# Mixer to MLP: x's first 512 columns are summed, weighted and turned while the output projection's second block runs

## The reference

```python
for l in range(2):
    h = rmsnorm(x, g_mix[l])
    # projections of h, three attention branches y_diff, y_mla, y_mem, and three gates
    merged = gates[:, :, 0] * y_diff + gates[:, :, 1] * y_mla + gates[:, :, 2] * y_mem
    x = x + merged @ w_out[l]                      # the output projection, 1024 x 1024

    u = rmsnorm(x, g_mlp[l]) @ w_mlp1[l]           # the MLP, 1024 x 4096
    x = x + jnp.square(jax.nn.relu(u)) @ w_mlp2[l]
```

## Time and profile before

| what | value |
|---|---|
| times of three executions | 2457.02, 2456.89, 2452.21 us |
| median | 2456.89 us |
| span of the profiled execution, first to last instruction | 2455.5 us |
| TensorE busy | 2387.7 us, 97% of the span |
| VectorE busy | 1521.6 us, 62% |
| ScalarE busy | 1188.3 us, 48% |
| GpSimd busy | 286.8 us, 12% |
| mean granted TensorE clock | 0.990 of full |

### The profile page before, as it was taken

How to read it: one execution, slowest core, us unless ns; L and a number is a source line. 1 busy time by engine, 2 the same in 40 slices (tenths; PEclk the granted TensorE clock), 3 DMA queues, 4 the chain that set the end, 5 groups by cost and what they waited for, 6 DMA issues and landing times.

```text
span 2455.5 us, 34969 instructions
## 1 busy us (share of the span) xinstructions
PE 2387.7 (97%) x14214; PEld 2058.1 (84%) x14214; DVE 1521.6 (62%) x2325; ACT 1188.3 (48%) x1782; POOL 286.8 (12%) x247
## 2 busy tenths in 40 slices
PE   8999999899999999999999999999999999999999
PEld 8987787689989977777899787787998877887997
DVE  6555556766556657666655677755665587656654
ACT  5444454344444445444444465554554455554543
POOL 1100010000000000000000122333100122333000
PEclk9999999999999999999999999999999999999999
DMA  7755645356656555544566655445566554445554
GB/s 231 210 190 174 166 119 150 118 154 189 184 172 185 181 192 174 169 141 153 165 181 204 197 162 147 125 125 163 177 193 210 182 163 125 126 139 162 174 187 146
DMA packets 269424, 411.69 MB, mean 168 GB/s; under 512 B 13770, under 2 KB 141658, under 8 KB 269264
## 3 DMA queue, kind: packets, MB, share of 16 engines
q1 hardware_dynamic: 262400, 389.59, 52.3%
q0 software_dynamic: 6432, 19.28, 3.0%
q10 hardware_dynamic: 432, 0.59, 0.1%
HBM read 408.31 MB, written 1.10 MB: 167 GB/s over the span
## 4 chain that ended last, share of the span: by engine, by line
PE 78%; DVE 13%; ACT 5%; issue 2%; POOL 1%; DMA 0%; SPq 0%; ACTq 0%; DVEq 0%
PE banks L1611 14%; PE banks L1613 14%; PE banks L1612 14%; PE banks L1637 10%; PE banks L1638 10%; PE banks L1646 9%; DVE w_lo L2192 3%; ACT w_hi L1890 3%; PE banks L1760 1%; PE banks L1700 1%; PE banks L1713 1%; DVE probs L2379 1%; DVE mx_merged L2867 1%; ACT probs L1998 1%; PE banks L1675 1%
## 5 line engine op out<-in xcount | busy, mean ns | idle before, releaser
L2192 DVE TENSOR_TENSOR w_lo<-w_raw,w_hi 128x1024 fp32r<-128x1024 f32 x688 | 838.7, 1224 | 690.4 <-ACT w_hi L1890 688.0
L1890 ACT ACTIVATE w_hi<-w_raw 128x1024 fp32r<-128x1024 f32 (+2 forms) x744 | 776.9, 1049 | 571.5 <-PE banks L1613 410.7
L1637 PE MATMUL banks<-xt_hi,w_hi 128*128 128x256 f32 x1920 | 479.4, 285 | 7.4 <-ACT xt_hi L1920 3.9
L1638 PE MATMUL banks<-xt_hi,w_lo 128*128 128x256 f32 x1920 | 477.9, 285 | 0.0
L1611 PE MATMUL banks<-w_hi,xt_hi 128*128 128x512 f32 (+2 forms) x1088 | 447.5, 411 | 11.5 <-DVE w_lo L2192 4.0
L1613 PE MATMUL banks<-w_hi,xt_lo 128*128 128x512 f32 (+2 forms) x1088 | 428.3, 394 | 0.0
L1612 PE MATMUL banks<-w_lo,xt_hi 128*128 128x512 f32 (+2 forms) x1088 | 427.4, 393 | 0.0
L1637 PEld LDWEIGHTS banks<-xt_hi,w_hi 128*128 128x128 f32 x1920 | 366.7, 191 | 10.0 <-issue 6.2
L1638 PEld LDWEIGHTS banks<-xt_hi,w_lo 128*128 128x128 f32 x1920 | 367.3, 191 | 0.0
L1646 PE MATMUL banks<-xt_lo,w_hi 128*128 128x256 f32 x1920 | 271.3, 283 | 0.0
L1611 PEld LDWEIGHTS banks<-w_hi,xt_hi 128*128 128x128 f32 x1088 | 206.7, 190 | 59.2 <-DVE w_lo L2192 6.4
(11 more groups left out here) (398 smaller groups left out, 2823.3 us busy)
## 6 DMA issues: line engine op xcount, KB each, us to landing
w_raw<-in_w_mlp SPq DMA_DIRECT2D x128, 512.0 KB, 3.7
w_raw<-in_w_in SPq DMA_DIRECT2D x104, 512.0 KB, 3.7
w_raw<-in_ffn_w_gate SPq DMA_DIRECT2D x88, 512.0 KB, 4.2
w_raw<-in_ffn_w_up SPq DMA_DIRECT2D x88, 512.0 KB, 4.3
w_raw<-in_ffn_w_down SPq DMA_DIRECT2D x88, 512.0 KB, 3.7
w_raw<-in_attn_w_in SPq DMA_DIRECT2D x72, 512.0 KB, 3.8
w_raw<-in_ret_w_in SPq DMA_DIRECT2D x64, 512.0 KB, 3.8
w_raw<-in_ret_w_out SPq DMA_DIRECT2D x16, 512.0 KB, 3.8
```

Source lines behind the costliest of these rows:

```text
L1637: pe.matmul(out[f], hi[:, cols], xh, start=(c == 0), stop=False)
L1638: pe.matmul(out[f], lo[:, cols], xh, start=False, stop=False)
L1890: act.activation(k.w_hi[i % SPLIT][:, 0:m], k.raw[i % RAW][:, 0:m], ACT.Copy).then_inc(*ev.mark(k.w_hi_made, ("w_hi", i)))
L2192: dve.tensor_tensor(lo, raw, hi.bitcast(F32), ALU.subtract).then_inc(*ev.mark(k.w_lo_made, ("w_lo", i)))
```

## The change

`last_plain` gets a mode `ahead`, used by the mixers only. In it the planner writes the steps of the next stage's first half between the tiles of the second block: behind T4 nothing, behind T5 the add and the gain of half 0, behind T6 the turn of half 0 and the add and the gain of half 1, behind T7 the turn of half 1. `feed` then finds that these are begun (`self.begun`) and starts at once with T8. So that the turned x can be written while T4 to T7 still read the turned merged rows, these lie in a place of their own (`mx_merged_t`, at 32 KiB of the work area, where the turned rows of the first branch lay before); they wait for the last tile that read these (`got["diff", "over"]`). No operation is added or removed, and the number of instructions is the same.

```diff
--- before.py
+++ after.py
@@ -456,7 +456,7 @@
         self.x_event = [[("x", 0, h, c) for c in range(2)] for h in range(HALVES)]
         self.tok_after = [[], []]
         self.xt, self.xt_after = None, []
-        self.pending, self.need_angles = None, True
+        self.pending, self.need_angles, self.begun = None, True, None
         self.memory, self.bias_heads, self.mem_after = None, {}, {}
         self.second_part = None
         self.out_scales, self.mem_scales, self.row_wide_of = {}, {}, {}
@@ -672,22 +672,23 @@
 
 
 
+    def begin(self, st):
+        return Transposed(f"x{st}", *self.xt_parts), self.next_gain(), {}
+
     def feed(self, between=None, order=""):
-        st, g = self.st, self.next_gain()
-        self.xt = Transposed(f"x{st}", *self.xt_parts)
+        st = self.st
+        begun, self.begun = self.begun, None
+        self.xt, g, gained = begun or self.begin(st)
         self.xt_scaled = True
-        gained = {}
 
         def part(half, c):
             if self.pending:
                 self.pending(half, c)
             by = "pool" if c and between else "dve"
-            self.step("gain", st, half, c, by, g, [self.x_event[half][c]] + self.tok_after[half])
-            gained[half, c] = "gain", st, half, c
+            self.gain_part(st, half, c, by, g, gained)
 
         def turned(half, c):
-            self.feed_turned = self.turn(lambda h, s: self.tok[:, h, s * P:(s + 1) * P], self.xt, half, [(4 * c + j, 4 * c + j) for j in range(4)],
-                                         [gained[half, c]], self.xt_after, order=order)
+            self.turn_part(self.xt, half, c, gained, order)
 
         def first():
             turned(0, 0)
@@ -710,6 +711,9 @@
             for half in range(HALVES):
                 self.step("rows", st, half, list(self.x_event[half]), self.stat(2), self.stat(1), self.row_means[half], "row_natural" if order else "row_scale")
 
+        if begun:
+            self.second_part = len(self.tiles) + 1, second
+            return
         part(0, 0)
         part(1, 0)
         if between:
@@ -720,6 +724,14 @@
                 self.held = list(range(SPLIT))
                 self.release(2)
             self.second_part = len(self.tiles) + 1, second
+
+    def gain_part(self, st, half, c, by, g, gained):
+        self.step("gain", st, half, c, by, g, [self.x_event[half][c]] + self.tok_after[half])
+        gained[half, c] = "gain", st, half, c
+
+    def turn_part(self, xt, half, c, gained, order=""):
+        self.feed_turned = self.turn(lambda h, s: self.tok[:, h, s * P:(s + 1) * P], xt, half, [(4 * c + j, 4 * c + j) for j in range(4)],
+                                     [gained[half, c]], self.xt_after, order=order)
 
     def last_tile(self):
         return "tile", len(self.tiles) - 1
@@ -764,19 +776,41 @@
             self.out_scales[st, half] = self.stat(1)
         return self.out_scales[st, half]
 
-    def last_plain(self, xt, w, rows, rows_out=False):
+    def last_plain(self, xt, w, rows, rows_out=False, ahead=False):
         st, out = self.st, []
-        for c, (c0, m) in enumerate(column_blocks(D)):
-            if c:
-                self.hold_last(rows * BLOCK // (P * TILE))
-            out.append((yield from self.block(xt, w, rows, c0, m)))
-        self.xt_after = [self.last_tile()]
 
         def update(half, c):
             self.step("add", st, half, c, ("blk", out[c].uid, half), self.x_event[half][c], rows_out)
             self.x_event[half][c] = "x", st + 1, half, c
 
+        def begin_next():
+            yield
+            self.begun = next_xt, g, gained = self.begin(st + 1)
+            for half in range(HALVES):
+                update(half, 0)
+                self.gain_part(st + 1, half, 0, "dve", g, gained)
+                yield
+                self.turn_part(next_xt, half, 0, gained)
+
         self.pending = update
+        out.append((yield from self.block(xt, w, rows, 0, BLOCK)))
+        self.hold_last(rows * BLOCK // (P * TILE))
+        if ahead:
+            side = begin_next()
+            tiles = self.block(xt, w, rows, BLOCK, BLOCK)
+            out.append((yield from self.both(tiles, side)))
+        else:
+            out.append((yield from self.block(xt, w, rows, BLOCK, BLOCK)))
+            self.xt_after = [self.last_tile()]
+
+    def both(self, tiles, side):
+        while True:
+            try:
+                state = next(tiles)
+            except StopIteration as stop:
+                return stop.value
+            next(side, None)
+            yield state
 
 
 
@@ -1333,6 +1367,7 @@
             yield from gate(2)
             self.xt_after = [self.last_tile()]
             yield from merge(0, 0, diff_t, "w_diff_o_2", D, 0)
+            got["diff", "over"] = self.last_tile()
             yield from merge(1, 2, mc_t, "w_cross_o_2", CROSS_H * CROSS_D, 4)
             yield from merge(2, 1, mc_t, "w_mla_o_2", MLA_H * MLA_V, 0)
 
@@ -1522,14 +1557,14 @@
         prepared = together(memory_keys(), diff_keys(), diff_queries(), latent(), latent_keys(), cross_queries(), diff_outputs())
         side = self.in_step(prepared, outputs())
         drive(projections(), side, finish=False)
-        merged_t = Transposed("merged" + L, *self.xt_parts)
+        merged_t = self.put_t("mx_merged_t" + L, 32, DC)
 
         for c in range(2):
             for half in range(HALVES):
                 self.turn(lambda h, s: merged[:, h, s * P:(s + 1) * P], merged_t, half, [(4 * c + j, 4 * c + j) for j in range(4)],
-                          [("merged", layer, half, c)], self.xt_after)
+                          [("merged", layer, half, c)], [got["diff", "over"]])
         self.tok_after = [[("turned", self.uid)]] * HALVES
-        drive(self.last_plain(merged_t, a["w_out_2"][layer], D))
+        drive(self.last_plain(merged_t, a["w_out_2"][layer], D, ahead=True))
```

## The result

The changed kernel takes 2457.6 us (median of 20 executions, 2456.7 to 2460.7), the kernel before 2453.9 us in the same comparison (20 executions, 2449.8 to 2458.6). The ratio is 1.0017, with a 95% interval of 1.0012 to 1.0023: 3 to 5.6 us slower (the two medians alone give 3.7). So the change is slower, clear of the scatter, by an amount that is most likely within the 0.2% (4.9 us) that the forecast called no change. The prediction was 2458.6 us, range 2452.5 to 2462.5.

What follows compares the result with a forecast made beforehand. TensorE bounds the kernel nearly everywhere, so only its waits count. Two places at 0.86 us gave 1.7 us, other terms nothing: span 2455.5 to 2457.2, plus 1.4 for the median, 2458.6 us; range 2452.5 to 2462.5.

Steps and rivals of the forecast that it cites:

- Placement (1): Turned merged rows in other buffers, last read long before: no instruction added, costed at nothing.
- Add, gain and turn of half 0 ahead (2, 3): Add and gain before T9's split on VectorE, four transposes (0.43 us) between T6 and T7: worth nothing alone.
- The gap's end (4): Between T7 and T8, half 1's gain is again held by GpSimd's T10 work: T8 starts 0.86 us later per place.
- 2.15 us of waits: TensorE's 3.02 us between T7 and T8, of which eight transposes at full clock take 0.87.
- The first rival: Half 1's gain starts before GpSimd's T10 work: T8 1.08 us earlier, 2454.7 us, or 2451.3 with the clock; chance 0.12.
- The clock (5): Half clock in T8 behind the new gap: bounds -1.72 to +1.72 us per place, taken as change 0.
- The price of a low stretch: T8 at half clock takes 4.60 us against 2.88 for a tile at full clock: 1.72 us.
- The base: Median of the three runs before, 1.4 us above the profiled span of 2455.5; that offset was kept.

Runs made afterwards that it cites:

- The filled kernels: Unread matmuls put into the waits between T7 and T8: in the changed kernel 2453.5 us (ratio 1.0000), in the kernel before 2452.1 us (0.9995).

## Why the prediction was right, and where it was off

- **Placement (1)**: worth nothing, as forecast; shown by the run with it alone.
- **Add, gain and turn of half 0 ahead (2, 3)**: worth nothing by themselves, as forecast; shown by the run with ScalarE's order put back.
- **The gap's end (4)**: forecast 0.86 us later per place through ScalarE's list, GpSimd's start and the held gain, with GpSimd 0.32 ahead. Measured 0.83 and 0.84, with GpSimd 0.33 ahead. Putting back ScalarE's order takes it away, and taking GpSimd off T10 takes 1.9 per place. This term is shown. The 2.15 us of waits that I counted in the old gap is also borne out: with both turns early T6 to T8 is 2.17 us shorter.
- **The first rival**, the gain ahead of GpSimd: did not come, but its price (1.08 less per place than before) is what the kernel with T10 on VectorE has: 4.78 against 5.84. That kernel reaches it by taking GpSimd's work away; no run shows the gain starting ahead of GpSimd's T10.
- **The clock (5)**: this is the term that was mis-sized. I took "the same 1.72 as before: change 0" from one profiled execution of before in which T8 ran at half clock at both places. That was one of the slower executions. In the profiles of kernels with before's waits of 1.77 us (0.98 and 0.78) the half clock came at 4 of 6 places; with the 2.6 us of the change at 4 of 4, once doubled; with 0.9 us or less, or none, or filled ones, at none of 16. The filled kernels size it by medians: 3.6 us in the change, 1.6 in the kernel before (one stretch per execution on average, at 1.5), so +2.0 us, where I had 0. With the 1.7 of step 4 that is 3.7, the measured difference. Each of these differences is uncertain by 1.3 to 2 us, so that +2.0 is a rough size. The mean clocks size it a second way, without the fills. Within the executions of one kernel the time falls by about 1.6 us per 0.001 of mean clock. The change's clock was 0.0018 lower in the first comparison (0.9899 against the 0.9917 that before had in the later sets; before's own clocks beside it are not known) and 0.0013 in the second: an estimate of 2.8 and 2.1 us. By means the change was 4.2 and 4.1 us slower, so 1.4 and 2.0 us are left for the later T8, on both sides of the 1.7 that step 4 gives. So that the change loses by its clock as well is shown; the split into 1.7 and 2 to 3 us is an estimate.
- **The price of a low stretch** is 1.5 us (5.23 against 3.74 from T8 to T9), not 1.72. I took T8's end from the chain, where the transposes behind it start at 1740.13; in the timeline of before they start at 1739.96. And I took 2.88 for a tile at full clock, where T8 itself takes 2.95 (1735.03 - 1732.08 with the placement alone). The two starts, in the timelines of TensorE of before and of the placement alone:

```profile
1739.96 1.04 PE L1700 MATMUL banks<-ident,tok 128*128 128x128 f32 x8
...
1735.03 1.03 PE L1735 MATMUL banks<-ident,tok 128*128 128x128 f32 x8
```

- **The base.** The median of three executions that I started from, 2456.9, was 3.0 above that of 20, 2453.9. Base and clock were off in opposite directions, which is why the forecast of 2458.6 came out 1.0 from 2457.6; the forecast difference was 1.7 and the measured one 3.7. The closeness of the two times is luck; the mechanism of step 4 is not.

What stays open: whether the waits ahead of T8 alone decide how often the clock falls, or also the pattern of the work in them. No run has the change's wait length with before's order. Nor do the runs show why the clock falls behind a given gap in one mixer and not in the other.

## What to carry to other kernels

Moving work ahead pays only if the last link of the chain moves; here the head start went to half 0, while half 1 set the gap, and the step put ahead in ScalarE's list delayed the GpSimd work that half 1 was stuck behind. When an operation takes several times as long as its sister of the same shape, look for the other engine's work that overlaps it, and either move one of them to where nobody waits or give it to the same engine. Where a gap is long enough for TensorE's clock to fall behind it, take the share of executions in which it falls from several profiles, not from one.

## What the runs showed of the hardware that was not expected

- A VectorE gain that is held by GpSimd's split ends 0.55 to 0.56 us behind the split's end whether it started 0.33 us after GpSimd (2.59 us long) or 1.77 us after it (1.17 us long).
- The same gap in the same program is followed by a stretch at half clock in one place and by none in another (3.74 and 5.24 us from T8 to T9 in one execution), and the stretch can begin ahead of T8, in the turn, and come twice in a row.
- Four matmuls that nobody reads, put into the waits, took 3.6 us off the change (by medians), while T8's start stayed at 6.67 us behind T6's end.
- One operation more on VectorE at each of the two places (T10's low half, 1.22 us) in place of 2.37 to 2.40 us on GpSimd, an engine that is busy for 12% of the span, took 2.8 us off the kernel before and 7 to 8 off the change. The work on the idle engine was the expensive one, because a gain that TensorE waited for stood behind it.
